# Hand-overs between latent stages: the first two chunks of the next stage multiplied in plain fp32

## The reference, cut to what matters

```python
def hybrid_layer(h, hc, ...):
    def pre(t, mm, i, gi):
        return rms_norm(t, g[gi]) * (1 + mm[:, :, i + 1]) + mm[:, :, i]
    def post(t, y, mm, i, gi, wres):
        return t + wres * mm[:, :, i + 2] * rms_norm(y, g[gi])
    h = post(h, swiglu(pre(h, m, 0, 0), ffn_wi[0], ffn_wo[0]), m, 0, 1, 0.5)      # ffn{l}a
    u = pre(h, m, 3, 2)
    o = latent_mix(u @ w_in, kv_c, cos, sin, qk_g, rpb, conv_w, rows)             # in{l}, attention
    h = post(h, o @ w_o, m, 3, 3, 1.0)                                            # attn_out{l}
    h = post(h, swiglu(pre(h, m, 6, 4), ffn_wi[1], ffn_wo[1]), m, 6, 5, 0.5)      # ffn{l}b
```

## Time and profile before

| | |
|---|---|
| median of 3 runs | 2904.39 us (2900.86 to 2908.22) |
| the profiled execution | 2902.97 us, its span 2901.1 us |
| granted TensorE clock, mean | 0.978 |
| PE, DVE, ACT, POOL busy | 97%, 61%, 40%, 6% |

### The profile page before, as it was taken

The page is one execution under the profiler, slowest core; times in us unless marked ns, Lnnn a source line. Parts: engine busy times, 40 slices in busy tenths (PEclk is TensorE's granted clock), DMA queues, the critical chain, the costliest instruction groups (busy, mean ns, idle before and its releaser), DMA issues.

```text
span 2901.1 us, 38832 instructions
## 1 busy us (share of the span) xinstructions
PE 2809.3 (97%) x16198; PEld 2321.0 (80%) x16198; DVE 1777.3 (61%) x2622; ACT 1160.7 (40%) x1558; POOL 161.6 (6%) x146
## 2 busy tenths in 40 slices
PE   6999999999999999999999998999999999999999
PEld 5887678786867787888888678888888888896998
DVE  4545449757643787746763477837668557656544
ACT  3343347534433575222342464222343222436544
POOL 0000000000000000000030122000030000301000
PEclk7999999999999999999999998999999999999999
DMA  7647789757377894534423112544425344241452
GB/s 293 257 188 300 257 300 368 296 204 305 132 271 275 336 356 173 194 133 161 151 102 105 49 45 73 186 137 164 152 88 203 131 163 162 98 138 59 145 184 107
DMA packets 77327, 539.68 MB, mean 186 GB/s; under 512 B 8688, under 2 KB 8944, under 8 KB 16736
## 3 DMA queue, kind: packets, MB, share of 16 engines
q1 hardware_dynamic: 75728, 530.92, 49.7%
q0 software_dynamic: 1424, 6.28, 0.9%
HBM read 536.12 MB, written 1.05 MB: 185 GB/s over the span
## 4 chain that ended last, share of the span: by engine, by line
PE 90%; DVE 5%; ACT 2%; DMA 1%; issue 1%; SPq 0%; POOL 0%; DVEq 0%; ACTq 0%
PE bank L1407 10%; PE bank L1408 10%; PE bank L1409 10%; PE bank L1091 8%; PE bank L1288 4%; PE bank L1442 4%; PE bank L1443 4%; PE bank L1444 4%; PE bank L1290 4%; PE bank L1289 4%; PE bank L1598 2%; PE bank L1313 2%; PE bank L1315 2%; PE bank L1280 2%; PE bank L1314 2%; PE bank L854 2%
## 5 line engine op out<-in xcount | busy, mean ns | idle before, releaser
L2355 DVE TENSOR_TENSOR w_lo<-raw,w_hi 128x2048 fp32r<-128x2048 f32 (+1 forms) x351 | 772.1, 2201 | 330.0 <-ACT w_hi L1799 329.2
L1799 ACT ACTIVATE w_hi<-raw 128x2048 fp32r<-128x2048 f32 (+1 forms) x351 | 644.7, 1839 | 488.7 <-PE bank L1444 207.2
L1407 PE MATMUL bank<-h_hi,w_hi 128*128 128x512 f32 (+1 forms) x1472 | 527.0, 358 | 12.5 <-DVE h_lo L2526 9.1
L1408 PE MATMUL bank<-h_lo,w_hi 128*128 128x512 f32 (+1 forms) x1472 | 524.3, 356 | 0.0
L1409 PE MATMUL bank<-h_hi,w_lo 128*128 128x512 f32 (+1 forms) x1472 | 524.3, 356 | 0.0
L1407 PEld LDWEIGHTS bank<-h_hi,w_hi 128*128 128x128 f32 x1472 | 280.7, 191 | 55.9 <-DVE h_lo L2526 8.2
L1409 PEld LDWEIGHTS bank<-h_hi,w_lo 128*128 128x128 f32 x1472 | 280.9, 191 | 38.7
L1408 PEld LDWEIGHTS bank<-h_lo,w_hi 128*128 128x128 f32 x1472 | 280.9, 191 | 38.3
L2407 DVE CUSTOM_DVE_ANT_0 bank<-raw,raw 128x1024 f32<-128x1024 f32 x240 | 286.4, 1256 | 0.0
L2097 ACT ACTIVATE quads<-bank 128x512 f32<-128x512 f32 (+1 forms) x88 | 47.9, 544 | 567.3 <-PE bank L1409 567.3
L1442 PE MATMUL bank<-act_hi,w_hi 128*128 128x512 f32 (+1 forms) x594 | 219.5, 370 | 0.0
(11 more groups left out here) (503 smaller groups left out, 4550.8 us busy)
## 6 DMA issues: line engine op xcount, KB each, us to landing
raw<-in_w_experts SPq DMA_DIRECT2D x192, 1024.0 KB, 6.3
raw<-in_w_ffn_in SPq DMA_DIRECT2D x88, 1024.0 KB, 4.8
raw<-in_w_mods SPq DMA_DIRECT2D x60, 1024.0 KB, 7.8
raw<-in_w_wide SPq DMA_DIRECT2D x60, 1024.0 KB, 4.8
raw<-in_w_ffn_out SPq DMA_DIRECT2D x48, 704.0 KB, 4.2
raw<-in_w_c_in SPq DMA_DIRECT2D x20, 1024.0 KB, 4.8
raw<-in_w_a_in SPq DMA_DIRECT2D x12, 1024.0 KB, 6.5
raw<-in_w_b_in SPq DMA_DIRECT2D x12, 1024.0 KB, 5.7
```

What stands on the lines that cost most here:

```text
L1407: pe.matmul(o, hi[:, f, :], h_hi[:, k, cols], start=(k == 0), stop=False)
L1408: pe.matmul(o, hi[:, f, :], h_lo[:, k, cols], start=False, stop=False)
L1799: act.activation(w_hi[pair_of(k)][:, 0:size], raw_of(k)[:, 0:size], ACT.Copy).then_inc(sem("hi_ready"), 1)
L2355: dve.tensor_tensor(w_lo[pair_of(k)][:, 0:size], raw_of(k)[:, 0:size], w_hi[pair_of(k)][:, 0:size].bitcast(F32), ALU.subtract).then_inc(*r ...
```

## The change

The first two chunks of in0, ffn0b, ffn1a and in1 are not split. PE multiplies them from the raw slot, as plain fp32, with an fp32 h that ACT writes into Y (made, raising h_made). The rounded copy h_hi (upper) and the rest h_lo (lower), which the later chunks need, are made from Y afterwards, for a pair of tiles in one instruction each. The raw slots of the two chunks are given back by PE's last product, no longer by DVE. keep_clock goes from 9 to 6 matmuls, the join pieces move two positions back, ACT's and DVE's orders are rewritten, and POOL's g_bias loads wait also for the last product that reads Y.

```diff
+        JOINED = ("in0", "ffn0b", "ffn1a", "in1")
+        unsplit = lambda name, c: name in JOINED and c < 2
...
                 pool.wait_ge(*W("h_ready", (KT // 2 - 1, 1), at=f"normin{l}"))
+                pool.wait_ge(*raw_done((f"in{l}", 1)))
...
-                later = {5: lambda: join.all_sums(1), 7: lambda: join.factor(1, "y"), 9: lambda: join.factor(1, "x")}
+                later = {7: lambda: join.all_sums(1), 9: lambda: join.factor(1, "y"), 11: lambda: join.factor(1, "x")}
...
-                keep_clock(psum[0], 9)
-                pe.wait_ge(*raw_done((name, 0)))
+                keep_clock(psum[0], 6)
+                pe.wait_ge(*raw_full((name, 0)))
...
-                            pe.wait_ge(*W("h_ready", (k // 2, x), at=norm))
+                            pe.wait_ge(*W("h_made", (k // 2, x), at=norm))
...
-                    for n, it in enumerate(ITEMS[name][c]):
-                        o, cut = psum[bank_of(name, c, n)][:, tok], slice(it[1], it[1] + P)
-                        pe.matmul(o, hi[:, k, cut], h_hi[:, k, tok], start=(k == 0), stop=False)
-                        pe.matmul(o, hi[:, k, cut], h_lo[:, k, tok], start=False, stop=False)
-                        out_.append(pe.matmul(o, lo[:, k, cut], h_hi[:, k, tok], start=False, stop=(k == KT - 1)))
-                    return out_
+                    w, tok = w3(raw_of((name, c)), KT), tokens((x,))
+                    return [pe.matmul(psum[bank_of(name, c, n)][:, tok], w[:, k, it[1]:it[1] + P], Y[:, k, tok], start=(k == 0), stop=(k == KT - 1))
+                            for n, it in enumerate(ITEMS[name][c])]
...
-                    if not (name == "attn_out0" and c == 3):
+                    if not (name == "attn_out0" and c == 3 or two and c < 2):
                         pe.wait_ge(*raw_done((name, c)))
...
+                def made(b, x):
+                    cols = tokens((x,))
+                    act.wait_ge(*W("normed", (b, x)))
+                    for k in (2 * b, 2 * b + 1):
+                        ins = act.activation(Y[:, k, cols], quad[k % 4][:, cols], ACT.Identity, bias=mod2[:, nl_of(norm), 3 * i_of(norm), k, x:x + 1])
+                    ins.then_inc(*T("h_made", (b, x), stage_of=norm))
+
+                def upper(b, x):
+                    both, cols = slice(2 * b, 2 * b + 2), tokens((x,))
+                    act.wait_ge(*W("h_made", (b, x), at=norm))
+                    act.activation(h_hi[:, both, cols], Y[:, both, cols], ACT.Copy).then_inc(*T("h_upper", (b, x)))
...
+                made(0, 0)
+                made(1, 0)
+                joint(name, 6, (1,))
+                made(2, 0)
+                joint(name, 7, (1,))
+                made(3, 0)
+                upper(0, 0)
+                root("y", 1)
+                upper(1, 0)
+                upper(2, 0)
+                root("x", 1)
+                upper(3, 0)
+                for b in range(KT // 2):
+                    made(b, 1)
+                for b in range(KT // 2):
+                    upper(b, 1)
...
-                        act.wait_ge(*W("product", (tag, c)))
+                        act.wait_ge(*(raw_done((name, at)) if unsplit(name, at) else W("product", (tag, c))))
...
-                        dve.wait_ge(*W("h_ready", (b - 2, x), at=norm))
+                        dve.wait_ge(*W("h_made", (b - 2, x), at=norm))
...
-                    split_lo((following, 0))
-                    lower(0, 0)
-                    part(6)
-                    scale(2, 0)
-                    normed(1, 0)
...
+                part(6)
+                scale(2, 0)
+                normed(1, 0)
+                part(7)
+                scale(3, 0)
+                normed(2, 0)
+                dot(6)
+                normed(3, 0)
+                dot(7)
+                inverse_y(1)
+                lower(0, 0)
+                new_squares(1)
+                lower(1, 0)
+                inverse_x(1)
+                lower(2, 0)
+                lower(3, 0)
+                scale(0, 1)
+                scale(1, 1)
+                add(0, 1)
+                normed(0, 1)
...
                 for b in range(KT // 2):
+                    lower(b, 1)
```

More of the change, by code:

```diff
@@ L1410, in up, with raw_up, marks @@
                     return mm
-                def marks(c, x, k, mm):
-                    if k == KT - 1 and x == streams(BEFORE[name])[-1]:
-                        mm.then_inc(*T("product", ("g0", c)))
+                def raw_up(c, x, k):
+                    w, cols = w3(raw_of((name, c)), 2 * KT), tokens((x,))
+                    return [pe.matmul(psum[2 * c + q][:, cols], w[:, q * KT + k, :], Y[:, k, cols], start=(k == 0), stop=(k == KT - 1))
+                            for q in range(2)]
+                def marks(c, x, k, last):
+                    if k == KT - 1 and x:
+                        last[1].then_inc(*raw_inc((name, c)))
                 def group(tag, back, first):
@@ L1887, in join @@
                 act.wait_ge(*W("mods", MODS_OF[norm], at="load"))
[L1888 to L1907, removed]
+                if split_from(name) == 4:
+                    joint(name, 5, (1,))
+                made(0, 0)
[14 more added lines that the diff above has]
+                    upper(b, 1)
             def head_pipe(name):
@@ L1946, in linear @@
                         if EVAC[name](c, n) == "evac_a":
-                            act.wait_ge(*W("product", (c, n)))
+                            act.wait_ge(*(raw_done((name, c)) if unsplit(name, c) and n else W("product", (c, n))))
                             evac(c, n).then_inc(*T("evac_a", (c, n)))
@@ L2523, in lower @@
                     dve.wait_ge(*W("h_upper", (b, x)))
[L2524 to L2529, removed]
+                    ins = dve.tensor_tensor(h_lo[:, both, cols], Y[:, both, cols], h_hi[:, both, cols].bitcast(F32), ALU.subtract)
                     ins.then_inc(*T("h_ready", (b, x), stage_of=norm))
@@ L2550, in join @@
                 scale(0, 0)
-                if two and split_from(name) == 4:
+                if split_from(name) == 4:
                     dot(5)
@@ L2555, in join @@
                 normed(0, 0)
-                if two:
-                    split_lo((following, 0))
-                    lower(0, 0)
-                    part(6)
-                    scale(2, 0)
-                    normed(1, 0)
[L2562 to L2565, removed]
-                    dot(6)
-                    normed(3, 0)
-                    lower(2, 0)
-                    dot(7)
-                    lower(3, 0)
-                    split_lo((following, 1))
-                    inverse_y(1)
-                    new_squares(1)
-                    inverse_x(1)
-                    scale(0, 1)
-                    scale(1, 1)
-                    add(0, 1)
-                    normed(0, 1)
-                for b in range(KT // 2):
-                    x = int(two)
-                    if b + 2 < KT // 2:
-                        scale(b + 2, x)
-                    if b + 1 < KT // 2:
-                        normed(b + 1, x)
-                    lower(b, x)
-                    if b == 0 and not two:
-                        split_lo((following, 1))
+                part(6)
[18 more added lines that the diff above has]
+                normed(0, 1)
+                for b in range(1, KT // 2):
+                    if b + 1 < KT // 2:
+                        scale(b + 1, 1)
+                    normed(b, 1)
+                for b in range(KT // 2):
+                    lower(b, 1)
                 stage[0] = now
```

35 lines of the change are left out of this document (8 added, 27 removed).

## The result

The changed kernel takes 2879.34 us (median of 4 runs, 2876.16 to 2881.53), the one before 2902.8 us in the same comparison (4 runs, 2900.86 to 2908.22). The ratio is 0.9913, 95% interval 0.9897 to 0.9928: 0.9% faster (the two medians alone give 0.8%). The prediction was 2889 us with a range of 2882 to 2902, so the direction was right and the gain larger than the range allowed. The profiled execution took 2879.47 us, its span 2877.6, 23.5 less than the span before.

A forecast was written before the change was run, and what follows sets the result against it. PE, busy 97% of the span, was taken as the bound. Four hand-overs fall from 149.8 to 130.8 us (-19.0), drops add 3.2: -15.8 from the median 2904.39 gives 2889 us, range 2882 to 2902.

The forecast's parts named there:

- Products: 64 per hand-over as plain fp32 matmuls, 0.436 us apart: 27.9 us a hand-over, 4.9 more than before.
- keep_clock 1.33: Cut from 9 to 6 matmuls in each hand-over: from 2.0 us to 1.33, so -0.67 each.
- PE's own work per hand-over: Products, keep_clock, all_sums(1) and two factors: 27.9 us before, 32.1 after, at full clock.
- No wait for w_lo: Sign to look for in the hand-overs: PE no longer waits for w_lo, which held it 1.79 us in the first.
- none for stream 1's h: Sign: PE never waits for stream 1's h, whose first pair had the thinnest cover, 0.6 us.
- no late load: Raw slots freed later delay no load; rival of late load or thin cover: 2893 to 2897 us, chance 0.03.
- w_lo alone holds PE for 1.79 us: Argument against the rival that the waits stay (+16.9, 2921 us, chance 0.07): w_lo holds PE 1.79 us, DVE 2.29.
- The term of drops: Half-rate stretches behind all_sums(1) in two of four hand-overs, 1.6 us lost each: +3.2 us.
- clean clock: Rival: all_sums(1) brings no clock drop, -19.0 us, 2885; with the forecast and the four-drops rival together, chance 0.72.
- The term of waits: Pair 3 of stream 0's h 0.2 to 0.5 us late; with a restart 0.6 us per hand-over.
- the best case, 2885: No clock drops behind all_sums(1) in the four hand-overs: -19.0 us; 3 us of scatter below gave the range's 2882.
- whose contrary I had left open at a chance of 0.03: Rival: fp32 passes don't hold PE's clock up, a product takes 0.87 us, possibly slower; chance 0.03.

The follow-up runs named there:

- a_lower_early: Kernel after, with stream 0's upper and lower put back between the pieces that make h: 2895.85 us, ratio 0.9977 to the kernel before.
- a_wait_all: Kernel after, with PE held until all four pairs of stream 0's h are made: 2910.38 us, ratio 1.0016 to the kernel before.
- b_tiny_split: Kernel before, with split_hi and split_lo of chunks 0 and 1 done on one column only: 2890.76 us, ratio 0.9948.
- b_early: Kernel before, with keep_clock no longer behind the wait for w_lo in in0 and in1: 2904.21 us, ratio 0.9998.
- b_fill: Kernel before, with keep_clock matmuls put where PE waits and none behind the w_lo wait in in0 and in1: 2896.63 us, ratio 0.9974.
- a_sums_plus12: Kernel after, with 12 more one-column matmuls ahead of those of all_sums(1): 2894.21 us, beside 2906.77 of the kernel before.
- a_sums2: Kernel after, with 6 more one-column matmuls ahead of those of all_sums(1): 2891.46 us, ratio 0.9954 to the kernel before.

## Why the prediction was right in kind and off in size

**Right.** Products: 0.436 us forecast, 27.8 us for 64 measured, which is 0.434. keep_clock 1.33 against 1.34. PE's own work per hand-over 32.1 against 31.9. No wait for w_lo, none for stream 1's h, no late load (chunk 2's first matmul has no bracket). The waits and the clock gave more back than the dearer products cost, as the sum said. Of the steps of the change this is now shown by undoing them: waits for h put back cost 17.3 us (a_lower_early), one long wait 28.8 (a_wait_all), and the split alone was worth 13.2 (b_tiny_split). These don't add up to the gain, since each moves the clock too.

**Two readings of before were off, without effect on the sum.** The wait for w_lo isn't in all four hand-overs. It stands in the first and fourth (in0 and in1), and b_early shows that it cost nothing of its own, so that "w_lo alone holds PE for 1.79 us" was no argument for the gain. And the 10.6 us behind the gaps are at 0.53, not 0.50, and hold the all_sums(1) of that hand-over, which starts at 1510.27 when the clock has already fallen.

**The term of drops was mis-sized.** The prediction says of half-rate stretches behind all_sums(1): "I count two of four: +3.2". There were none, 0 us. I had carried a case of all_sums(0) over to all_sums(1), although the row nearest to it, 1.00 across all_sums(1) itself in the last hand-over the earlier trace rows, spoke for none. The rival "clean clock" had this right. The runs with longer sums show that the step wasn't foolish, since with 0.7 us more the count is two of four, but for the kernel as it stands it is wrong. Behind all_sums(0), with the same small matmuls among trios, the kernel after has its half-rate stretch in the first and fourth hand-over and none in the third. In the second the drop begins with all_sums(0) itself, which here stands behind a wait:

```profile
1742.89 0.94 PE L967 MATMUL bank<-ones,zeroc 1*128 1x4 f32 x4 [2.95 <-DVE joint L2448]
```

Behind all_sums(1) the count is three of nine among trios (b_fill and the others above), and none of 20 among plain products with the same sums. That speaks for the neighbours having a part in it. It isn't shown: in b_fill the waits ahead of the sums differ as well, and no run exchanged the products alone.

**The term of waits was mis-sized.** "With a restart I count 0.6 us each", 2.4 in all, for a pair 3 of h that would be 0.2 to 0.5 us late. It was 0. ACT's timeline in the first hand-over after, the pieces that set it:

```profile
1500.47 0.91 ACT L1874 ACTIVATE y_out<-quads,mod_lat 128x256 f32<-128x256 f32 x2 [0.74 <-DVE quads L2510]
1501.29 0.40 ACT L1851 ACTIVATE joint<-y_out 128x256 f32<-128x256 f32 x1
...
1502.26 0.42 ACT L1856 ACTIVATE joint<-y_out 128x256 f32<-128x256 f32 x1
1502.58 0.89 ACT L1874 ACTIVATE y_out<-quads,mod_lat 128x256 f32<-128x256 f32 x2
1503.38 0.40 ACT L1851 ACTIVATE joint<-y_out 128x256 f32<-128x256 f32 x1
...
1504.36 0.42 ACT L1856 ACTIVATE joint<-y_out 128x256 f32<-128x256 f32 x1
1504.69 0.91 ACT L1874 ACTIVATE y_out<-quads,mod_lat 128x256 f32<-128x256 f32 x2
```

Where ACT goes from one finished input to the next, each piece starts 0.09 to 0.1 us before the one ahead of it ends (1501.38 to 1501.29, 2.68 to 2.58, 3.47 to 3.38, 4.78 to 4.69). I had added durations where I should have added distances between starts, as I had done for PE. Four such seams make 0.4 us: pair 3 is made 6.5 us after PE's old work ends and not 7.0, and PE wants it at 6.7 (12 products of 0.447 behind 1500.42 is 1505.8; the pair ends at 1505.60). The cover is 0.2 us, so that nothing was waited for is in part luck: it rests on a margin that the sum could not have resolved.

**The sum of the misses.** Profile against profile I forecast -15.8 and got -23.5. Drops 3.2, waits 2.4 and own work 0.9 (128.4 for the four against 127.54) make 6.5. The remaining 1.2 lie outside the hand-overs, where single stretches moved by up to 1.9 us either way with no edit in them. Two of these go with the clock. Between the second and third hand-over the span is 1.6 us shorter, and the stretch behind all_sums(0) is at half rate before (first row) and not after (second):

```profile
2136.50:2139.90 3.40, 3.40 (x19) 0.50 0.01 2
2123.30:2126.70 3.40, 3.40 (x32) 1.00 0.00 0
```

Behind the last hand-over it is 1.6 us shorter too, and there another half-rate stretch lasts from 2628.0 to 2634.8 before and from 2606.6 to 2610.0 after. The 1.9 us more ahead of the first I don't explain. The other 2 us of the 9.7 between 2889 and 2879.34 are the median of before, taken 1.4 above its profiled execution when after's fell on its own, and 0.4 of rounding.

**The range was cut too near on the good side.** It set 3 us of scatter below the best case, 2885. All three of the small terms went the same way, and the two larger ones, drops and waits, came out at zero together. The low end should have taken drops and waits as zero together on the profiled execution's own time (2902.97 less 19.0 less 2.4 is 2881.6), and then gone below by the scatter.

**The clock.** Here the trace shows 0.50 behind a long gap (a_wait_all), behind gaps and small matmuls together and behind small matmuls alone (a_sums_plus12), and 1.00 in 32 us of plain fp32 passes without gaps. The Trainium skill (TensorE: Matmul & The Clock Gate, Part 1: The HAM clock gate) says that recent activity decides the throttle. The runs agree with it as to the direction; that the clock stays up through plain fp32 passes, whose contrary I had left open at a chance of 0.03, is what the four rows at 1.00 show.

## What to carry to other kernels

An operand path that costs more on the bound engine can still win, if what it replaces is a chain that this engine waits for, and if those waits cost clock beside their own length. Price such a step from the whole hand-over, width against own work against clock, and add the feeding engine's pieces by distances between starts. A cover of 0.2 us and a clock that fell in two of four hand-overs with 0.7 us more of small matmuls are thin: whoever adds a piece to either must read the windows again.

## What the runs showed of the hardware

- A plain fp32 product of 128x128 by 256 columns takes 0.427 to 0.447 us in dense work, the trio of split matmuls 0.36 us: a fifth more, and the weight needs no split on DVE and ACT.
- The same gaps do not always have the same price: in b_tiny_split three hand-overs stayed at 1.00 and one fell to 0.82, 6 us longer.
- The stretch ahead of the first hand-over, which no edit touched, ended between 1491.6 and 1500.5 us in eleven profiled executions. In b_fill, a_sums2 and a_lower_early it was 6.5 to 7.5 us shorter than in after. Most of this is the clock: from 140 to 260 us it is 0.91 in after and 0.94 in b_fill, and from 560 to 580 us 0.91 and 1.00, which by width times (1 - clock) is some 5 us of the 7.5. Only the windows around the edit can be compared between single executions; the whole span can't at this size.
